# Later one-time buffers for expert weights, and one modulation group summed on VectorE, in a two-layer mixer and mixture-of-experts kernel

## The reference, cut to what matters

```
mod = silu(c) @ w_mod[l] + b_mod[l]            # 1024 x 6144 weights a layer
x = x + gt1 * rmsnorm(token_mixers(h, hc, ...) @ w_out, g_post1[l])
aff = softmax(h2 @ w_router); g, idx = top_k(aff over tokens, 32)     # per expert
hid = silu(xs @ w1[e]) * (xs @ w3[e]);  y = hid @ w2[e] * g           # 16 experts
x = x + gt2 * rmsnorm(scatter_add(y), g_post2[l])
```

## Time and profile before

| | us |
|---|---|
| median of 3 runs (1985.23, 1988.09, 1988.78) | 1988.09 |
| the profiled execution's own time | 1984.07 |
| its span, first to last instruction | 1982.1 |
| PE busy | 1706.7 |
| DVE busy | 526.5 |
| ACT busy | 325.6 |
| HBM read | 522.70 MB |

### The profile page before, as it was taken

How to read it: one execution, slowest core, us unless ns; L and a number is a source line. 1 busy time by engine, 2 the same in 40 slices (tenths; PEclk the granted TensorE clock), 3 DMA queues, 4 the chain that set the end, 5 groups by cost and what they waited for, 6 DMA issues and landing times.

```text
span 1982.1 us, 21707 instructions
## 1 busy us (share of the span) xinstructions
PE 1706.7 (86%) x9211; PEld 883.4 (45%) x9211; DVE 526.5 (27%) x1022; ACT 325.6 (16%) x776; POOL 93.5 (5%) x171
## 2 busy tenths in 40 slices
PE   6999999999998998979888799999996666666665
PEld 2656444444476332424222266857884323223222
DVE  2145044354613111112111513344113101011102
ACT  4123144200023100101001321243012000000001
POOL 5000110000012000000000000110000000000000
PEclk9999999999999999999999999999998767777776
DMA  9310104543536899999999931105746999999996
GB/s 344 112 43 22 16 1 191 213 170 130 188 151 233 363 422 421 422 421 422 421 421 421 396 118 44 37 1 174 252 168 240 421 421 421 421 421 421 420 422 253
DMA packets 130668, 525.17 MB, mean 265 GB/s; under 512 B 9886, under 2 KB 73532, under 8 KB 75276
## 3 DMA queue, kind: packets, MB, share of 16 engines
q1 hardware_dynamic: 127884, 520.47, 66.2%
q0 software_dynamic: 2688, 3.32, 0.9%
HBM read 522.70 MB, written 1.05 MB: 264 GB/s over the span
## 4 chain that ended last, share of the span: by engine, by line
PE 57%; DMA 36%; DVE 4%; ACT 1%; issue 1%; SPq 0%; DVEq 0%; ACTq 0%
DMA ring<-in_w_e_dram 35%; PE ps L780 13%; PE ps L1040 9%; PE ps L1220 7%; PE ps L1049 4%; PE ps L1079 4%; PE ps L1004 3%; PE ps L690 2%; PE ps L966 2%; PE ps L1172 2%; PE ps L882 2%; PE ps L1242 1%; PE ps L1200 1%; DMA ring<-in_w_mod_dram 1%; PE ps L988 1%; PE ps L859 1%
## 5 line engine op out<-in xcount | busy, mean ns | idle before, releaser
L1220 PE MATMUL ps<-ring,arena 128*32 128x256 f32 (+1 forms) x2912 | 395.3, 519 | 118.5 <-DMA ring<-in_w_e_dram 114.9
L1220 PEld LDWEIGHTS ps<-ring,arena 128*32 128x32 f32 (+1 forms) x2912 | 126.5, 131 | 372.8 <-DMA ring<-in_w_e_dram 199.0
L1242 PE MATMUL ps<-ring,arena 128*32 128x256 f32 (+1 forms) x1536 | 217.6, 550 | 77.8 <-DMA ring<-in_w_e_dram 74.1
L1040 PE MATMUL ps<-arena,ring 128*128 128x512 f32 (+1 forms) x576 | 191.8, 486 | 0.0
L780 PE MATMUL ps<-arena,ring 128*128 128x512 f32 (+1 forms) x480 | 175.2, 523 | 1.4 <-DVE arena L1781 1.4
L1242 PEld LDWEIGHTS ps<-ring,arena 128*32 128x32 f32 (+1 forms) x1536 | 70.2, 138 | 221.0 <-issue 108.2
L1585 ACT ACTIVATE arena<-ps 128x512 f32<-128x512 f32 (+1 forms) x32 | 15.7, 490 | 797.8 <-PE ps L1220 797.8
L2003 DVE COPY arena<-ps 32x512 f32<-32x512 f32 (+1 forms) x128 | 70.9, 554 | 273.2 <-PE ps L1242 271.9
L1040 PEld LDWEIGHTS ps<-arena,ring 128*128 128x128 f32 x576 | 109.1, 190 | 76.1 <-issue 68.6
L780 PEld LDWEIGHTS ps<-arena,ring 128*128 128x128 f32 x480 | 90.2, 190 | 82.5 <-issue 76.6
L1996 DVE TENSOR_TENSOR arena<-arena,ps 128x512 f32<-128x512 f32 (+1 forms) x32 | 17.7, 555 | 368.8 <-PE ps L1220 368.8
(11 more groups left out here) (211 smaller groups left out, 1406.6 us busy)
## 6 DMA issues: line engine op xcount, KB each, us to landing
ring<-in_w_e_dram SPq DMA_DIRECT2D x372, 1024.0 KB, 17.8
ring<-in_w_mod_dram SPq DMA_DIRECT2D x48, 1024.0 KB, 9.7
ring<-in_w_in_dram SPq DMA_DIRECT2D x44, 1024.0 KB, 10.1
arena<-in_w_e_dram SPq DMA_DIRECT2D x10, 1024.0 KB, 11.8
ring<-in_w_out_dram SPq DMA_DIRECT2D x8, 1024.0 KB, 11.8
arena<-in_w_br_ml_dram SPq DMA_DIRECT2D x8, 512.0 KB, 6.4
arena<-in_w_br_mla_dram SPq DMA_DIRECT2D x8, 256.0 KB, 4.0
arena<-in_w_br_na_dram SPq DMA_DIRECT2D x8, 256.0 KB, 4.9
```

Source lines behind the costliest of these rows:

```text
L1040: mm = pe.matmul(ps[:, u % 3, tq], wg[:, k, cols], hT[:, k, tq], start=k == 0, stop=k == KD - 1)
L1220: mm = pe.matmul(ps[M * j:M * j + M, m, 0:NW], XSTs[l][e // GROUP % 2][:, kk, e % GROUP, 0:M], w[:, k, j * NW:(j + 1) * NW], start=kk == 0 ...
L1242: mm = pe.matmul(ps[M * j:M * j + M, 3, 0:NW], lhs, w[:, k, j * NW:(j + 1) * NW], start=kk == 0, stop=kk == KD - 1)
```

## The change

`SPARE` names other loads and more buffers, all from load 8 on: 8 in layer 0 and 12 in layer 1. Loads 0 to 7 go through the ring in both layers. The issue order interleaves them by the time at which their buffers come free. Group 4 of the modulation leaves the ring: its 8 loads go through the four `mix` buffers, DVE multiplies and adds them (`mod4_part`) into four accumulators of 512 columns, between the `post` steps of layer 0's output projection, and 4 `pick` matmuls on PE finish it.

```diff
-    if layer == 0:
-        loads += [("mod", *MOD_GROUPS[4], k) for k in range(KD)]
...
-SPARE = [{0: "mix0", 1: "mix1", 2: "mix2", 3: "mix3"},
-         {0: "ctx_rows", 1: "mixer_consts", 2: "branch0", 7: "mix0", 8: "mix1", 9: "mix2", 10: "mix3", 11: "merged_end"}]
+SPARE = [{8: "mix0", 9: "mix1", 10: "mix2", 11: "mix3", 12: "ya0", 13: "ya1", 14: "yg", 15: "xst1"},
+         {8: "ctx_rows", 9: "mixer_consts", 10: "old_rows", 11: "ya0", 12: "mix0", 13: "mix1", 14: "mix2", 15: "yg",
+          16: "mix3", 17: "merged_end", 18: "ya1", 19: "gains"}]
+SPARE_ORDER = [[8, 9, 10, 11, 12], [13, 14, 15], [8, 9, 10, 11], [12, 13, 14, 16], [17, 18, 15, 19]]
...
     if l == 0:
-        return order[:-4] + experts[:4] + order[-4:] + experts[4:]
-    return order[:-4] + experts[:2] + order[-4:] + experts[2:]
+        mods = [(("mod4", l, k), None) for k in range(KD)]
+        order += mods[:4] + experts[:4] + mods[4:] + pick(SPARE_ORDER[0]) + experts[4:8] + pick(SPARE_ORDER[1]) + experts[16:]
+        return order
+    return order[:-4] + pick(SPARE_ORDER[2][:3]) + order[-4:] + pick(SPARE_ORDER[2][3:]) + experts[:4] + pick(SPARE_ORDER[3]) + \
+        experts[4:8] + pick(SPARE_ORDER[4]) + experts[20:]
...
                 if name[:3] == "mix" and name[3:].isdigit():
                     sp.wait_ge(sem("mg_branch"), before("mg_branch", l) + 24)
+                    if l == 0:
+                        sp.wait_ge(sem("mod_part"), 2 * KD + 4 + int(name[3:]) + 1)
...
-                elif name == "branch0":
-                    sp.wait_ge(sem("mg_branch"), before("mg_branch", l) + 18)
+                elif name == "old_rows":
+                    sp.wait_ge(sem("mod_tr"), 6)
+                elif name == "ya0":
+                    if l:
+                        sp.wait_ge(sem("mg_branch"), before("mg_branch", l) + 18)
+                    else:
+                        sp.wait_ge(sem("x_post1"), 2)
+                elif name in ("ya1", "gains"):
+                    sp.wait_ge(sem("x_post1"), before("x_post1", l) + layers[l].nt)
+                elif name == "yg":
+                    sp.wait_ge(sem("n2_rstd"), before("n2_rstd", l) + layers[l].nt)
+                    sp.wait_ge(sem("mod_summed"), 3)
+                elif name == "xst1":
+                    sp.wait_ge(sem("logit_parts"), before("logit_parts", l) + layers[l].nt)
...
+                    if kind == "mod4":
+                        sp.wait_ge(sem("mg_branch"), 24)
+                        if a[0] >= 4:
+                            sp.wait_ge(sem("mod_part"), 2 * KD + a[0] - 3)
+                        g = MOD_GROUPS[4][1]
+                        sp.dma_start(spare_slots[f"mix{a[0] % 4}"], w_mod[1, a[0] * P:(a[0] + 1) * P, g * SLOT:(g + 1) * SLOT])\
+                            .then_inc(sem(f"weights_landed_mix{a[0] % 4}"), 16)
+                        continue
...
-                pool.wait_ge(sem("x_post1"), before("x_post1", l) + L.nt)
-                pool.memset(Ya[:, 4 - L.nt:4, :], 0.0).then_inc(sem("ya_added"), 1)
...
                     pool.nop().then_inc(sem("weighted"), 1)
+                    if g == 0:
+                        pool.wait_ge(used, expert_load(l, 1, 1, 3) + 1 if l == 0 else expert_load(l, 0, 2, 3) + 1)
+                        pool.memset(Ya[:, 4 - L.nt:4, :], 0.0).then_inc(sem("ya_added"), 1)
...
                 if l == 0:
-                    for k in range(3):
-                        mod_product(4, k)
+                    pe.wait_ge(sem("mod_part"), 3 * KD)
+                    pe.wait_ge(sem("mod_row"), 4)
+                    for j in range(4):
+                        mm = pe.matmul(ps[32 * j:32 * j + 32, 6, :], pick[:, 1, :], mod4_acc[j], start=True, stop=True)
+                    mm.then_inc(sem("mod_summed"), 1)
...
-                if l == 0:
-                    for k in range(3, KD):
-                        mod_product(4, k)
...
+            def mod4_part(k):
+                s_ = f"mix{k % 4}"
+                w = spare_slots[s_]
+                dve.wait_ge(sem(f"weights_landed_{s_}"), 16 * (k // 4 + 1))
+                dve.wait_ge(sem("mod_part"), 2 * KD + k)
+                for j in range(4):
+                    cols = slice(512 * j, 512 * j + 512)
+                    if k:
+                        ins = dve.scalar_tensor_tensor(out=mod4_acc[j], in0=w[:, cols], scalar=cT[:, k, 1:2], in1=mod4_acc[j],
+                                                       op0=ALU.mult, op1=ALU.add)
+                    else:
+                        ins = dve.tensor_scalar(mod4_acc[j], w[:, cols], cT[:, k, 1:2], None, ALU.mult)
...
                 for j, t in enumerate(L.chunks[:-1]):
+                    if l == 0:
+                        for k in ((0, 1, 2, 3), (4, 5), (6, 7))[j]:
+                            mod4_part(k)
                     post(1, j, t, Ym, G1, tmp1)
```

More of the change, by code:

```diff
@@ L196 @@
     _n += len(ring_loads(_l)) + len(EXPERT_LOADS)
-SPARE = [{0: "mix0", 1: "mix1", 2: "mix2", 3: "mix3"},
-         {0: "ctx_rows", 1: "mixer_consts", 2: "branch0", 7: "mix0", 8: "mix1", 9: "mix2", 10: "mix3", 11: "merged_end"}]
+SPARE = [{8: "mix0", 9: "mix1", 10: "mix2", 11: "mix3", 12: "ya0", 13: "ya1", 14: "yg", 15: "xst1"},
+         {8: "ctx_rows", 9: "mixer_consts", 10: "old_rows", 11: "ya0", 12: "mix0", 13: "mix1", 14: "mix2", 15: "yg",
+          16: "mix3", 17: "merged_end", 18: "ya1", 19: "gains"}]
+SPARE_ORDER = [[8, 9, 10, 11, 12], [13, 14, 15], [8, 9, 10, 11], [12, 13, 14, 16], [17, 18, 15, 19]]
 SLOT_OF, PREVIOUS, USE = [], [], []
 def _assign_slots():
-    turn, last, count = 0, {}, {}
+    turn, last, count = 0, {}, {f"mix{i}": 2 for i in range(4)}
     for l in range(2):
@@ L229, in issue_order, with pick @@
     experts = [(("expert", l, *a), j) for j, a in enumerate(EXPERT_LOADS)]
+    def pick(js):
+        return [experts[j] for j in js]
     if l == 0:
-        return order[:-4] + experts[:4] + order[-4:] + experts[4:]
-    return order[:-4] + experts[:2] + order[-4:] + experts[2:]
+        mods = [(("mod4", l, k), None) for k in range(KD)]
[3 more added lines that the diff above has]
+        experts[4:8] + pick(SPARE_ORDER[4]) + experts[20:]
 def expert_load(l, e, m, q):
@@ L257, in backbone, with gate_row @@
         ring = sb("ring", SLOTS, SLOT)
[L258 to L261, removed]
+        rows = sb("rows", 7, 512)
+        mod_tmp, b_row, g_row = (rows[:, i, :] for i in (4, 5, 6))
+        def gate_row(l, g):
+            return rows[:, 2 - 2 * l + (g - 1 if l == 0 else 2 - g), :]
         ident = sb("ident", P)
@@ L345, in backbone @@
         junk_y = view(12288, D)
-        hot, Sr, Sg = (view(19968 + 512 * b, 2, 2, P) for b in range(3))
+        hots, Srs, Sgs = ([view(19968 + 512 * b, 2, 2, P), view(19200 + 256 * b, 1, 2, P)] for b in range(3))
+        mod4_acc = [view(at, 512) for at in (13312, 13824, 21504, 22912)]
         XTs = [view(8192, 4, KD, P), view(6144, 4, KD, P)]
@@ L352, in backbone @@
         Ya = view(14336, 4, D)
-        sgh = view(18432, 512)
-        hid = view(18944, 512)
-        hidT = view(19456, 512)
+        sghs, hids, hidTs = ([view(18432 + 512 * b, 512), view(18432 + 256 * b, 256)] for b in range(3))
         G2s = [view(8192, 2, D), view(7168, 2, D)]
@@ L384, in backbone @@
                        "ctx_rows": X[:, 0:2, :].rearrange("p a d -> p (a d)"), "mixer_consts": mixer_consts[:, 0:SLOT],
-                       "branch0": view(14336, SLOT), "merged_end": view(10240, SLOT)}
+                       "old_rows": rows[:, 2:6, :].rearrange("p a n -> p (a n)"),
+                       "ya0": view(14336, SLOT), "ya1": view(16384, SLOT), "yg": view(12288, SLOT),
+                       "xst1": view(10240, SLOT), "merged_end": view(10240, SLOT), "gains": view(19968, SLOT)}
         def w_slot(n):
@@ L666, in _ @@
                             g_ = aff[:, c2 * L.ns + si, GROUP * g:GROUP * (g + 1)].rearrange("p (e j) -> p e j", j=1)
-                            own(pool.tensor_tensor(Sg[:, si, c2, :].rearrange("p (e j) -> p e j", e=GROUP),
-                                                   hot[:, si, c2, :].rearrange("p (e j) -> p e j", e=GROUP),
+                            own(pool.tensor_tensor(Sgs[l][:, si, c2, :].rearrange("p (e j) -> p e j", e=GROUP),
+                                                   hots[l][:, si, c2, :].rearrange("p (e j) -> p e j", e=GROUP),
                                                    g_.to_broadcast([P, GROUP, CAP]), ALU.mult))
                     pool.nop().then_inc(sem("weighted"), 1)
+                    if g == 0:
+                        pool.wait_ge(used, expert_load(l, 1, 1, 3) + 1 if l == 0 else expert_load(l, 0, 2, 3) + 1)
+                        pool.memset(Ya[:, 4 - L.nt:4, :], 0.0).then_inc(sem("ya_added"), 1)
                 if l == 0:
@@ L731, in mod_turn @@
                 l, g = MOD_GROUPS[o]
-                src = mod_tmp[:, :] if g == 0 else gate_rows[:, 2 * l + g - 1, :]
+                src = mod_tmp[:, :] if g == 0 else gate_row(l, g)
```

(31 more changed lines are left out.)

## The result

The change takes 1967.86 us (median of 4 runs, 1965.12 to 1971.78) against 1986.78 us before (4 runs, 1985.23 to 1988.78): a ratio of 0.9906, 95% interval 0.9885 to 0.9927. The forecast was 1968, from 18.5 us of gain; measured are 18.9. The profiled execution took 1965.12 us, its span is 1963.2.

The account below looks back on a forecast made before the run. Four parts in a row bound it: mixer 0 (PE), expert loads (DMA), mixer 1 (PE), a second load stream. Gains of 12.6 (layer 1), 5.9 (layer 0) and 0 (group 4), 18.5 us, from 1986.5 give 1968; range 1960 to 1976.

Parts of the forecast that it names:

- (restart) + 2.49 us a load: Expert streams of both layers: each ends at its restart plus 2.49 us per load left, plus an unchanged tail.
- Layer 1: Layer 1's expert stream: restart at 1516.1 us with load 20, whose old turn was 1528.7; gain 12.6 us.
- Layer 0: Layer 0's expert stream: an earlier restart alone would give 16.9 us; after ring starvation 5.9 us of gain is left.
- both holes: Layer 0's stream: DMA stands still 8.5 us from 666.7, and again at gather 1, from 695.1 until load 32 at 697.6.
- no starvation: Layer 0's stream: loads flow as in layer 1, 16.9 us there, 29.5 in all, time 1957; chance 0.06.
- the rival in which waits of PE take layer 0's gain: Layer 0, 645 to 697 us: PE waits for DVE, ACT or POOL take all 5.9; time 1974; chance 0.09.
- Group 4 at 0: Layer 0 before the experts: DVE work covered, 0.9 us gained on PE against 0.6 of colder gather 0; taken as 0.
- The cold rival: Layer 0: clock stays low through gather 0 into the first loads, 5.8 us later; gain 13.6, time 1973; chance 0.08.

Follow-up runs that it names:

- e1: The change's layer 1 buffers only, layer 0 and group 4 as in the kernel before: 0.9939 of before, 1972.88 us.
- e4: Only group 4 moved to the mix buffers and DVE, expert loads of both layers as in the kernel before: 0.9985 of before.
- e2: Layer 0 as in the change, layer 1 with the old buffers and order of the kernel before: 0.9959 of before, 1976.98 us.
- e5: The change with each part of group 4 in 16 DVE passes of 128 columns instead of 4 of 512: one run, 1969.67 us.
- e8: The change itself run again, on the chip of the other runs: 0.9906 of before, 1967.29 us.
- e3: The change with layer 0's 8 one-time buffers holding loads spread from 15 to 52 instead of 8 to 15: 0.9849 of before, 1956.27 us.
- e6: The kernel of e3 plus 7 (layer 0) and 4 (layer 1) unused matmuls on PE before gather 0: 0.9841 of before, 1953.93 us.
- e7: The kernel of e3 run again, beside the change on one chip: 0.9837 of before, 1954.54 us.

## Why the prediction was right

**Both streams are (restart) + 2.49 us a load.** Layer 1: forecast 12.6, measured in D 12.4 (mean of 429.8, 430.3 and 429.3 against seven values of 417.0 to 417.6). Layer 0: forecast 5.9, measured in B 444.1 (before, e1, e4) less 437.8 (the change, e2, e5, e8), 6.4, with both holes at the forecast places: from the first expert matmul the reloads came at + 1.9 us (forecast 1.9), load 24 at + 30.2 (30.3), load 32 at + 52.3 (52.7). What the rival "no starvation" gave, 16.9, is what e3 measures when the holes are taken away: 17.0 (444.1 less 427.1). So the step that set layer 0's gain, ring slots that stand full while PE reads one-time buffers, is shown from both sides.

**No chain took the place of the DMA wait.** PE ran from 642.06 to 713.24 with no wait of note, so nothing speaks for the rival in which waits of PE take layer 0's gain.

**Group 4 at 0: right in its smallness, wrong inside.** I set 0.9 us of gain on PE against 0.6 us of a colder gather 0. The gain came (0.6 to 0.9), the loss did not in the change's profile: gather 0 took 9.28 us against 9.30. From the 1.00 just ahead of the gather I took it that a 0.50 there would cost more than before. But before, the granted clock fell right behind that row, inside the gather: it averages 0.72 over 636 to 642 us (first line, before). In the change it was at 0.50 from 626 us on, and it rose again 3.3 us into the gather (second line, after).

```profile
636.00:642.00 6.00, 6.00 (x40) 6.00 (x40) 0.89 (x4) 1.50 (x4) 3.27 (x6) 0.72 1.02 419
...
632.00:642.00 10.00, 9.23 (x66) 9.11 (x66) 2.73 (x7) 3.72 (x11) 4.87 (x10) 0.79 0.02 4
```

Both gathers lost some 1.7 us by it (6 x 0.28 before, half of 3.3 after): in the change the clock fell 10 us earlier, but that time lay in PE's wait and not in the gather. Over the profiles without extra matmuls gather 0 ran from 9.14 to 10.37, so the loss depends on when in it the clock rises. The cold rival (15.1 us) is out. That idle gaps of PE let the clock fall (the Trainium skill, TensorE: Matmul & The Clock Gate, "HAM oscillation") agrees in kind with e6: busy PE, 1.00, 7.80 us.

**What I had not in the sum.** The two profiles differ by 18.9, but not by my terms alone: start 2.0, A 0.9, B 7.4, C -3.1, D 12.2, E -0.4. The 2.0 and the -3.1 are the clock again. Before, a stretch at half speed lay in mixer 0 (166 to 190 us: 0.93; after: 1.00). The change run again (e8) had no such stretch in mixer 0, and its output projection started earlier still, at 548.4. After, two lay at the end of layer 0's experts, which made `expert_out` of the last expert 8.8 us instead of 7.1 and four scatter matmuls 3.5 instead of 2.0:

```profile
1088.00:1096.00 8.00, 5.73 (x24) 2.27 (x22) 2.75 (x4) 1.88 (x2) 0.00 (x0) 0.84 1.01 422
1104.00:1112.00 8.00, 7.97 (x15) 3.59 (x16) 4.25 (x7) 3.56 (x9) 0.00 (x0) 0.80 1.01 420
```

C is 425.3 or 425.4 in four profiles, among them before and e3, and 428.5 to 430.7 in five, of which three (e5, e7, e8) have a stretch of low clock elsewhere, between 1292 and 1315 us. That one comes and goes with the same kernel (e3 and e7). Of the two at the end of layer 0's experts, both came in the change and e2, only the first in e8 (`expert_out` of 8.80 us in all three), and neither in e5. So they are no fixed cost of the change. But none of the six profiles with other buffers in layer 0 has the first one, so whether the change's layout makes it likelier is open. The Trainium skill, in the same page's "What's actually happening", calls the number of slow matmuls at a start run-variable; the profiles here show it of stretches in the middle too. That my gain met the measured one within 0.4 us is therefore partly luck, with 2.0 us one way and 3.1 the other in a single pair of profiles that no term of mine stood for.

## What to carry to other kernels

When a stream of transfers bounds a stage, its end is the time of its restart plus the transfer time of what is left, so count the loads in memory at that time and find the first slot that is used. Memory that can be filled only once should hold loads that are used late and far apart, not the next ones: while PE reads a run of one-time buffers, no slot comes free and the stream stops. Another layout of the same 8 buffers was worth 11 us here, more than the 6.4 that the change gained in layer 0's stream. One spread layout was tried; whether a better one exists is not shown.

## What was not expected of the hardware

The granted clock fell to half for some 3 us (0.84 and 0.80 over 8 us above) or some 7 (e7, 0.57 over 1292 to 1300 us) at places that differ from execution to execution of one kernel, and each such place on the path moved the time by 1.5 us (four scatter matmuls) to 3.7 us (C of e7 against e3). A part of 2048 columns took 2.79 us of DVE in 4 passes and 4.34 in 16, so a pass costs about 0.13 us beside its columns in this place; the estimate of 0.75 us for 512 columns was 0.70.
